# A hybrid attention step on one core: one input tile requested earlier, and the first gated tiles prepared ahead of weight splits

## The chip, the cores and the metric

The kernel runs on one core of a Trainium2 chip. The metric is the device time of one execution in microseconds. The median of the kernel before is 1729.63 us over 3 runs (1727.05 to 1729.91).

## What is computed

One layer of a decoder step in float32, for a prompt of 1024 rows and for 8 x 8 sampled rows. All rows are normalised and multiplied by one wide input matrix. Branch A is windowed attention in three dilations, branch B differential attention. Each branch output is gated, projected to 1024 columns, the projections are merged by sigmoid gates, and a last projection and the residual follow:

```python
h = rms_norm(x, norm_g); z = h @ w_in          # q, k, v of both branches, gates ga, gb, ma, mb
o_a = combine_groups(outs, lses)               # three dilated windows, weighted by their softmax sums
o_b = rms_norm(o_b, subln_g) * (1.0 - lam_init)
ya = o_a * silu(ga); yb = o_b * silu(gb)
pa = ya @ w_proj_a;  pb = yb @ w_proj_b
m = sigmoid(ma) * pa + sigmoid(mb) * pb
y = x + m @ w_out
```

## The kernel before

The program is written out by hand for each engine: five instruction streams (SP for transfers, GpSimd, ScalarE, VectorE, TensorE), ordered among themselves by semaphores only. An engine works strictly in the order of its stream, so an instruction that waits holds all that stand behind it. Rows come in 9 tiles: eight of 128 prompt rows (0 to 7) and one of the 64 sampled rows (8).

**Products in three parts.** A float32 product is made from rounded high and low parts: `hi*w_hi`, `hi*w_lo`, `lo*w_hi` (L2000 to L2002, and L2052 to L2054 for the gate units). So each weight chunk, 128 x 512 and 256 KB, is loaded into one of four `raw` buffers, ScalarE rounds it to `w_hi` (`split_hi`, L1195), and GpSimd (`split_lo`, L985) or VectorE (L1513) subtracts to make `w_lo`. A raw buffer is loaded again only when the `w_lo` of the chunk four before is done; in the late part of the kernel it is ScalarE that waits for this and issues the load (L1187, L1188), right behind a split.

**The start.** Chunks 0 to 7 are those of the first block of input weights. An input tile goes: load into one of two `xt` buffers (L704, `load_x`), `Square` with a row sum on ScalarE (L1206), reciprocal root on GpSimd (L965, L966), scaling on VectorE (`rows_scale`, L1520), eight transposes on TensorE (L1948), gain on VectorE (`hn`, L1529), high part on ScalarE (L1182), low part on GpSimd (L972). `load_x(i)` for i >= 2 waits until `rows_scale(i - 2)` is done. SP's order is: tile 0, two constants, tile 1, chunks 0 to 3, tile 2, chunks 4 to 7 (each behind the `w_lo` of the chunk four before), four small `qcol` loads, then, in `block_io(0)`, one tile and one chunk of the next block in turn, starting with tile 3. VectorE's order there is: `w_lo` of chunk 4, `rows_scale(2)`, `w_lo` of chunks 5 to 7, `rows_scale(3)`, `input_gain(2, 0)`; ScalarE's: split of chunks 4 to 7, square of tile 3, the high parts of tile 2. The second half of tile 2 is transposed by TensorE behind the first tile's products; that transposition waits for `input_gain(2, 0)`.

**The seam.** The decode part runs over groups `gg` = 0 to 70 (`SLOTS` is 70), and between its pieces the gate units (0 to 59) are multiplied. The last units stand at the end: in `gg` = 70 TensorE does unit 57, transposes `zyA` of tile 0 (`turn_y(0, 0)`, L1980), does unit 58, transposes `zyB` of tile 0, does unit 59 (16 products, the sampled rows), and goes on to `project(0, 0)`. From there its order is, for each tile i: `project(0, i)`, `turn_y(0, i+1)`, `project(1, i)`, `turn_y(1, i+1)`, with the transposes of the merged rows (`turn_m`) behind it.

In groups 64 to 69 two chunks a group of the projection weights are split (`late_splits`); those of `w_proj_a` have their low part made on VectorE, the first four of `w_proj_b` on GpSimd, in groups 68 and 69; chunk 4 of it stands ahead of unit 57. Chunks 5, 6, 7 of `w_proj_b` and the first of `w_out` (here called chunks 5 to 8) come behind group 70; 5 and 7 belong to GpSimd, 6 and 8 to VectorE.

The gated rows of a tile are prepared in two branches. Branch a: three attention outputs `ogA` and the gate `sgA` are loaded (L895, L900); GpSimd weights two of them and adds (`y_prepare_a`, L1110 twice, L1112), VectorE weights the third, adds and multiplies by the gate (`y_a`, L1764, L1766, L1770), which gives `zyA`. Branch b: `ogB` and `sgB` are loaded; ScalarE squares (`square`, L1388), GpSimd multiplies by the norm's weight and makes the reciprocal root (`y_prepare_b`, L1117, L965, L966), VectorE reduces, scales and multiplies by the gate (`y_b`, L1775, L1778, L1781), which gives `zyB`. After the transposition ScalarE moves the high part (`move_y`, L1392) and VectorE makes the low part (`y_low`, L1785), on which `project` waits. SP loads the pieces of the next tile of a branch when `zyA` or `zyB` of the one before is done (`load_y`). VectorE multiplies the projections by the merge gates (`gated`, L1806), two steps for each tile and branch.

Of the kernel before, what the change touches and what calls it, by code (L numbers as in the profile page):

```python
# [133 lines left out]
def build_step(nc, x_p, x_s, ca, cb, page_table, norm_g, w_in, qna, kna, qnb, knb, lq1, lk1, lq2, lk2,  # L134
# [17 lines left out]
    with ExitStack() as ctx:  # L152
# [378 lines left out]
        def splits_at(gg):  # L531

            return [q for q in sorted(split_slot) if split_slot[q] == gg]
# [162 lines left out]
        def _(sp):  # L696
# [22 lines left out]
            load_x(2)  # L719
            for k in range(4, KC):  # L720
                load_chunk(0, k)
            for col, vec in ((0, qna), (1, qnb)):
                for h in range(2):
                    sp.dma_start(qcol[h * HD:(h + 1) * HD, col:col + 1],
                                 vec[0].rearrange("(d o) -> d o", o=1)).then_inc(s_const, 16)
# [9 lines left out]
            def block_io(u):  # L735
                kind, G = U[u][0], U[u][1]
                for i in range(TILES):
                    if u == 0 and 3 <= i + 3 < TILES:
                        load_x(i + 3)
                    if u == 0 and i == NT - 1:  # L740
                        constants()
                    if i < KC:
                        load_chunk(u + 1, i)
                    if kind == "k":
                        kk = TILES * G + i
                        dst = kept(G, i, 0) if i < NT else kept_new(G, 0)
                        if dst is not None:
                            sp.wait_ge(kn_ready, kk + 1)
                            sp.dma_start(dst, kn[0:nrows(i), kk % 3, :])\
                                .then_inc(k_out[kk % 3], 16)  # L750
                            if i == NT:
                                sp.dma_start(new_scr[0, :, (G - 1) % 4], kn[0:NS, kk % 3, :])\
                                    .then_inc(k_out[kk % 3], 16)
                    if kind == "v" and G == 0 and i == NT:
                        sp.wait_ge(lo_done, first_chunk[4])
                        table_b(0)
                        table_b(1)
                    if kind == "v" and G and i == 5:
                        sp.wait_ge(k_out[2], k_sent[2][TILES * G + NT])
                        table_in(G, 0)  # L760
                    if kind == "v":
                        dst = kept(G, i, 1) if i < NT else kept_new(G, 1)
                        if dst is not None:
                            sp.wait_ge(v_ready, TILES * G + i + 1)
                            sp.dma_start(dst, v_sb[0:nrows(i), i, :]).then_inc(v_out, 16)
                            if i == NT:
                                sp.dma_start(new_scr[1, :, (G - 1) % 4], v_sb[0:NS, NT, :]).then_inc(v_out, 16)
# [184 lines left out]
        def _(pool):  # L952
# [183 lines left out]
            for gg in range(SLOTS + 1):  # L1136
# [6 lines left out]
                if n == 4 and b + 1 < DEC_B:  # L1143
# [1 line left out]
                    pool.wait_ge(*lo_ready(last_split[0]))  # L1145
                    queries(b + 1, slice(2, 4)).then_inc(s_qa, 1)
                    pool.wait_ge(s_qa, b + 2)
                if gg == SLOTS - 1:
                    y_prepare_a(0)
                for q in (*splits_at(gg), *late_splits(gg)):  # L1150
                    if not by_vector(q):
                        split_lo(*divmod(q, KC))
                if gg == SLOTS:
                    y_prepare_b(0)
                for m in gates_at(gg):
                    splits_for(m)
            def splits_of(chunks):
# [2 lines left out]
                        split_lo(*divmod(q, KC))  # L1160

            y_prepare_a(1)
            splits_of(range(Q_PB + NC + SPARE, Q_OUT + SPARE))
            for i in range(TILES):
                if i + 1 < TILES:
                    if i:
                        y_prepare_a(i + 1)
                    y_prepare_b(i + 1)
                if i:
                    merge(i - 1)  # L1170
# [7 lines left out]
        def _(act):  # L1178
# [228 lines left out]
            for gg in range(SLOTS + 1):  # L1407
# [38 lines left out]
                if gg == N_GROUPS + 3:  # L1446
                    act.wait_ge(ew_exp, 1)
                    act.activation(ew[:, :, :, :], ew[:, :, :, :], ACT.Exp).then_inc(ew_exp, 1)
                for q in splits_at(gg):
                    split_hi(*divmod(q, KC))  # L1450
                if gg == SLOTS:
                    act.wait_ge(s_pu, 9 * DEC_B)
                    square(0)
                for m in gates_at(gg):
                    gate(m)
                    if gg == SLOTS and m < GATE_UNITS - 1:
                        move_y(m - (GATE_UNITS - 3), 0)
                for q in late_splits(gg):
                    split_hi(*divmod(q, KC))
            for q in range(Q_PB + NC + SPARE, Q_OUT + SPARE):  # L1460
                split_hi(*divmod(q, KC))

# [7 lines left out]

            for i in range(TILES):
                if i + 1 < TILES:
                    square(i + 1)
                    move_y(0, i + 1)
                else:
                    halves(i, 0)
# [23 lines left out]
        def _(dve):  # L1500
# [397 lines left out]
                        split_lo(*divmod(q, KC))  # L1898

            y_a(1)  # L1900
            splits_of(range(Q_PB + NC + SPARE, Q_OUT + SPARE))
            for i in range(TILES):
                if i:
                    gated(1, i - 1)
                if i + 1 < TILES:
                    if i:
                        y_a(i + 1)
                    y_b(i + 1)
                gated(0, i)
                if i + 1 < TILES:  # L1910
# [506 lines left out]
```

## Time and profile before

| | |
|---|---|
| median of 3 runs | 1729.63 us (1727.05 to 1729.91) |
| the profiled execution, its own time | 1733.43 us |
| its span | 1731.6 us |
| TensorE products, busy | 1641.2 us (95%) |
| VectorE / GpSimd / ScalarE busy | 723.8 / 664.3 / 602.0 us |
| mean granted clock of TensorE | 0.987 |

The span is the profiled stretch from its first to its last instruction; the execution's own time has a little more around it. Matmuls are pipelined and overlap, so a busy TensorE is not one at its peak. The granted clock is 1.00 at 2.4 GHz and 0.50 at 1.2 GHz; a window that has both shows a mean. An idle time in brackets is that of the engine just before the instruction, with the step that ended it.

### The profile page before, as it was taken

How to read it: one execution, taken by the hardware profiler on the slowest of the kernel's cores; microseconds unless marked ns; L12 is line 12 of the kernel's file. 1: busy time of each engine (PE TensorE's matmuls, PEld its weight loads, DVE VectorE, ACT ScalarE, POOL GpSimd, SP SyncE). 2: the span in 40 equal slices, each digit the busy share in tenths (PEclk: the TensorE clock that was granted, in tenths of full speed). 3: DMA queues.
4: the chain of work that ended last, by engine and by line, in shares of the span. 5: the costliest groups of instructions: out<-in, count | busy, mean ns of one | idle time of the engine just before them, and what ended most of it. 6: DMA issues, size and time to landing. Idle time of an engine off the chain costs nothing.

```text
span 1731.6 us, 38772 instructions
## 1 busy us (share of the span) xinstructions
PE 1641.2 (95%) x14872; PEld 1406.5 (81%) x14872; DVE 723.8 (42%) x1788; ACT 602.0 (35%) x1405; POOL 664.3 (38%) x958
## 2 busy tenths in 40 slices
PE   6999888999999999999999999999999899999998
PEld 5888565778799999899998887777777788878787
DVE  5521556322174221642216463444354342478511
ACT  4422465422164221642217243334243344311300
POOL 5666110257452475524656131211221111466500
PEclk9999999999999999999999999999999999999999
DMA  5164710564814667344532789989899887755422
GB/s 159 56 221 160 251 51 0 164 202 170 272 50 135 205 232 245 116 158 163 195 114 70 257 274 297 309 281 320 277 317 310 279 284 236 256 182 177 151 91 79
DMA packets 184062, 336.27 MB, mean 194 GB/s; under 512 B 29969, under 2 KB 74130, under 8 KB 177746
## 3 DMA queue, kind: packets, MB, share of 16 engines
q1 hardware_dynamic: 143586, 221.68, 39.4%
q10 hardware_dynamic: 40304, 112.22, 19.2%
q8 instruction: 117, 1.92, 0.4%
q14 instruction: 55, 0.45, 0.1%
HBM read 294.05 MB, written 127.07 MB: 243 GB/s over the span
## 4 chain that ended last, share of the span: by engine, by line
PE 89%; issue 3%; DMA 2%; ACT 2%; DVE 2%; SPq 1%; POOL 1%; ACTq 0%; DVEq 0%; POOLq 0%
PE ps L2000 14%; PE ps L2002 14%; PE ps L2001 14%; PE ps L2052 5%; PE ps L2053 5%; PE ps L2054 5%; PE ps L2207 4%; PE ps L2151 4%; PE ps L2100 4%; PE ps L2171 3%; PE ps L2266 3%; PE ps L2249 2%; PE ps L2158 2%; PE ps L2121 2%; PE ps L1969 2%
## 5 line engine op out<-in xcount | busy, mean ns | idle before, releaser
L985 POOL TENSOR_TENSOR w_lo<-raw,w_hi 128x512 fp32r<-128x512 f32 x140 | 180.2, 1293 | 446.5 <-ACT w_hi L1195 445.9
L2000 PE MATMUL ps<-w_hi,hT 128*128 128x512 f32 x824 | 341.0, 414 | 2.0 <-POOL hT L972 1.0
L2002 PE MATMUL ps<-w_hi,hT 128*128 128x512 f32 x824 | 330.5, 401 | 0.0
L2001 PE MATMUL ps<-w_lo,hT 128*128 128x512 f32 x824 | 330.2, 401 | 0.0
L2000 PEld LDWEIGHTS ps<-w_hi,hT 128*128 128x128 f32 x824 | 206.2, 250 | 21.2 <-issue 1.4
L2052 PE MATMUL ps<-w_hi,hT 128*128 128x256 f32 x768 | 221.8, 289 | 1.6 <-issue 1.2
L2053 PE MATMUL ps<-w_lo,hT 128*128 128x256 f32 x768 | 217.2, 283 | 6.2 <-issue 6.2
L2002 PEld LDWEIGHTS ps<-w_hi,hT 128*128 128x128 f32 x824 | 206.5, 251 | 20.5
L2001 PEld LDWEIGHTS ps<-w_lo,hT 128*128 128x128 f32 x824 | 206.8, 251 | 18.1
L2054 PE MATMUL ps<-w_hi,hT 128*128 128x256 f32 x768 | 216.7, 282 | 0.0
L1195 ACT ACTIVATE w_hi<-raw 128x512 fp32r<-128x512 f32 x158 | 98.8, 629 | 200.2 <-DMA raw<-in_w_in 185.4
L2052 PEld LDWEIGHTS ps<-w_hi,hT 128*128 128x128 f32 x768 | 147.2, 192 | 9.9 <-issue 9.1
L2053 PEld LDWEIGHTS ps<-w_lo,hT 128*128 128x128 f32 x768 | 147.3, 192 | 3.6 <-issue 3.6
L2054 PEld LDWEIGHTS ps<-w_hi,hT 128*128 128x128 f32 x768 | 147.0, 191 | 3.2 <-issue 3.2
L1719 DVE STREAM_TRANSPOSE k_in<-k_in 128x512 f32<-128x512 f32 x224 | 138.1, 677 | 1.8 <-DMA k_in<-in_cache_a_kv 1.7
L1038 POOL TENSOR_SCALAR qz<-qT 64x128 f32<-64x128 f32 x208 | 109.2, 525 | 63.4 <-PE ps L2151 52.1
L966 POOL TENSOR_TENSOR rs<-ss,half_pow 128x8 f32<-128x8 f32 (+3 forms) x81 | 127.0, 1568 | 6.7
L1584 DVE TENSOR_REDUCE ss<-ps 128x8 f32<-128x512 f32 (+1 forms) x72 | 49.7, 690 | 172.1 <-ACT ps L1265 172.1
L1265 ACT ACTIVATE ps<-ps 128x512 f32<-128x512 f32 (+1 forms) x72 | 41.8, 580 | 213.6 <-PE ps L2002 206.2
L1597 DVE TENSOR_TENSOR zn<-ps,rs 128x512 f32<-128x512 f32 (+1 forms) x72 | 49.7, 690 | 141.9 <-POOL rs L966 141.9
L2151 PE MATMUL ps<-kT,qz 128*128 128x128 f32 (+1 forms) x384 | 101.3, 350 | 5.0 <-POOL qz L1038 3.5
L1326 ACT ACTIVATE sA<-sA,st_sum 128x128 f32<-128x128 f32 (+1 forms) x192 | 86.2, 449 | 42.5 <-DVE st_sum L1685 36.6
(233 smaller groups left out, 2863.1 us busy)
## 6 DMA issues: line engine op xcount, KB each, us to landing
out<-in_cache_a_kv ACTq DMA_DIRECT2D x29, 2040.0 KB, 9.3
k_in<-in_cache_b_kv SPq DMA_DIRECT2D x128, 256.0 KB, 3.8
v_in<-in_cache_b_kv SPq DMA_DIRECT2D x128, 256.0 KB, 6.2
raw<-in_w_in SPq DMA_DIRECT2D x104, 256.0 KB, 4.1
k_in<-in_cache_a_kv SPq DMA_DIRECT2D x104, 256.0 KB, 6.5
v_in<-in_cache_a_kv SPq DMA_DIRECT2D x104, 256.0 KB, 6.7
out<-in_cache_a_kv ACTq DMA_DIRECT2D x7, 2016.0 KB, 8.9
raw<-in_w_in ACTq DMA_DIRECT2D x40, 256.0 KB, 5.7
```

Of the source, the lines that this page charges most:

```text
L966: return pool.tensor_tensor(out, in_, half_pow[0:r, 0:heads], ALU.pow)
L985: pool.tensor_tensor(lo, raw_of(q), hi.bitcast(F32), ALU.subtract).then_inc(lo_done, 1)
L1038: return pool.tensor_scalar(out, in_, 1.0, None, ALU.mult)
L1195: act.activation(weights(q)[0], raw_of(q), ACT.Copy).then_inc(hi_done, 1)
L1719: dve.transpose(k_in[:, gg % NKS, j, :], k_in[:, gg % NKS, j, :]).then_inc(s_kt, 1)
L2000: pe.matmul(z, hi, wh, start=first, stop=False)
L2001: pe.matmul(z, hi, wl, start=False, stop=False)
L2002: return pe.matmul(z, lo, wh, start=False, stop=last)
L2052: pe.matmul(part, hi, wh, start=k == 0, stop=False)
L2053: pe.matmul(part, hi, wl, start=False, stop=False)
L2054: ins = pe.matmul(part, lo, wh, start=False, stop=k == KC - 1)
L2151: pe.matmul(bank(s % 4)[:, 0:W], qz[:, hh, i * P:(i + 1) * P], kT[:, k0:k0 + W], start=True, stop=True).then_inc(aq, 1)
```

## The change

Three engines and SP get another order; no instruction is added and none removed.

- SP: `load_x(3)` is issued behind chunk 5 of the first block, ahead of chunks 6 and 7 and of the `qcol` loads. `block_io(0)` then begins its tiles with 4.
- GpSimd: `y_prepare_a(0)` moves from group 69 to group 68, and in either group it stands ahead of that group's splits. `y_prepare_b(0)` stays in group 70 and is written ahead of that group's splits. `y_prepare_b(1)` moves ahead of the splits of chunks 5 to 8, to where `y_prepare_a(1)` already stands.
- ScalarE: in group 70, `square(0)` is written ahead of the splits; `square(1)` moves ahead of the splits of chunks 5 to 8.
- VectorE: `y_b(1)` moves ahead of the splits of chunks 5 to 8, behind `y_a(1)`.

```diff
--- before.py
+++ after.py
@@ -719,6 +719,8 @@
             load_x(2)
             for k in range(4, KC):
                 load_chunk(0, k)
+                if k == 5:
+                    load_x(3)
             for col, vec in ((0, qna), (1, qnb)):
                 for h in range(2):
                     sp.dma_start(qcol[h * HD:(h + 1) * HD, col:col + 1],
@@ -735,7 +737,7 @@
             def block_io(u):
                 kind, G = U[u][0], U[u][1]
                 for i in range(TILES):
-                    if u == 0 and 3 <= i + 3 < TILES:
+                    if u == 0 and 4 <= i + 3 < TILES:
                         load_x(i + 3)
                     if u == 0 and i == NT - 1:
                         constants()
@@ -1145,13 +1147,13 @@
                     pool.wait_ge(*lo_ready(last_split[0]))
                     queries(b + 1, slice(2, 4)).then_inc(s_qa, 1)
                     pool.wait_ge(s_qa, b + 2)
-                if gg == SLOTS - 1:
+                if gg == SLOTS - 2:
                     y_prepare_a(0)
+                if gg == SLOTS:
+                    y_prepare_b(0)
                 for q in (*splits_at(gg), *late_splits(gg)):
                     if not by_vector(q):
                         split_lo(*divmod(q, KC))
-                if gg == SLOTS:
-                    y_prepare_b(0)
                 for m in gates_at(gg):
                     splits_for(m)
             def splits_of(chunks):
@@ -1160,11 +1162,11 @@
                         split_lo(*divmod(q, KC))
 
             y_prepare_a(1)
+            y_prepare_b(1)
             splits_of(range(Q_PB + NC + SPARE, Q_OUT + SPARE))
             for i in range(TILES):
-                if i + 1 < TILES:
-                    if i:
-                        y_prepare_a(i + 1)
+                if 0 < i < TILES - 1:
+                    y_prepare_a(i + 1)
                     y_prepare_b(i + 1)
                 if i:
                     merge(i - 1)
@@ -1446,17 +1448,18 @@
                 if gg == N_GROUPS + 3:
                     act.wait_ge(ew_exp, 1)
                     act.activation(ew[:, :, :, :], ew[:, :, :, :], ACT.Exp).then_inc(ew_exp, 1)
-                for q in splits_at(gg):
-                    split_hi(*divmod(q, KC))
                 if gg == SLOTS:
                     act.wait_ge(s_pu, 9 * DEC_B)
                     square(0)
+                for q in splits_at(gg):
+                    split_hi(*divmod(q, KC))
                 for m in gates_at(gg):
                     gate(m)
                     if gg == SLOTS and m < GATE_UNITS - 1:
                         move_y(m - (GATE_UNITS - 3), 0)
                 for q in late_splits(gg):
                     split_hi(*divmod(q, KC))
+            square(1)
             for q in range(Q_PB + NC + SPARE, Q_OUT + SPARE):
                 split_hi(*divmod(q, KC))
 
@@ -1470,7 +1473,8 @@
 
             for i in range(TILES):
                 if i + 1 < TILES:
-                    square(i + 1)
+                    if i:
+                        square(i + 1)
                     move_y(0, i + 1)
                 else:
                     halves(i, 0)
@@ -1898,13 +1902,13 @@
                         split_lo(*divmod(q, KC))
 
             y_a(1)
+            y_b(1)
             splits_of(range(Q_PB + NC + SPARE, Q_OUT + SPARE))
             for i in range(TILES):
                 if i:
                     gated(1, i - 1)
-                if i + 1 < TILES:
-                    if i:
-                        y_a(i + 1)
+                if 0 < i < TILES - 1:
+                    y_a(i + 1)
                     y_b(i + 1)
                 gated(0, i)
                 if i + 1 < TILES:
```

## Rows read from the trace of the kernel before

**Rows 1.** The page's chain that ended last: shares of the span by engine.

```profile
PE 89%; issue 3%; DMA 2%; ACT 2%; DVE 2%; SPq 1%; POOL 1%; ACTq 0%; DVEq 0%; POOLq 0%
```

**Rows 2.** Windows of the start: busy time of each engine, granted clock (PEclk).

```profile
25.00:30.00 5.00, 2.06 (x9) 1.73 (x10) 2.04 (x3) 1.79 (x5) 2.04 (x3) 0.90 0.64 214
30.00:35.00 5.00, 5.00 (x23) 4.07 (x21) 3.03 (x4) 2.64 (x5) 4.71 (x5) 0.76 0.15 59
```

**Rows 3.** Timeline of the start: start us, length us, engine, line, instruction, [idle before <-releaser].

```profile
12.86 4.89 SPq L711 DMA_DIRECT2D raw<-in_w_in  x4
...
20.31 0.58 SPq L704 DMA_DIRECT2D xt<-in_x_prompt  x1
...
20.33 2.96 DVE L1513 TENSOR_TENSOR w_lo<-raw,w_hi 128x512 fp32r<-128x512 f32 x3
...
20.41 0.63 ACT L1195 ACTIVATE w_hi<-raw 128x512 fp32r<-128x512 f32 x1 [0.76 <-DMA raw<-in_w_in]
...
24.34 1.06 ACT L1206 ACTIVATE xn<-xt 128x1024 f32<-128x1024 f32 x1 [3.30 <-DMA xt<-in_x_prompt]
...
26.44 0.75 DVE L1520 TENSOR_SCALAR xn<-xt,rs_x 128x1024 f32<-128x1024 f32 x1 [3.15 <-POOL rs_x L966]
...
27.94 0.63 PE L1948 MATMUL ps<-ident,xn 128*128 128x128 f32 x4 [3.43 <-DVE hn L1529]
```

**Rows 4.** Windows of TensorE alone: products before and behind the seam's waits, with PEclk.

```profile
1485.49:1491.36 5.87, 5.86 (x49) 1.00 0.59 175
1495.91:1503.70 7.79, 7.79 (x52) 0.73 0.89 298
1511.78:1517.62 5.84, 5.84 (x27) 1.00 0.69 246
1521.83:1530.23 8.40, 8.40 (x26) 0.66 0.77 263
```

**Rows 5.** Timeline of the seam, GpSimd, VectorE, ScalarE, SP and TensorE.

```profile
1474.42 0.39 SPq L900 DMA_DIRECT2D sgA<-g_scr  x1
...
1485.49 2.61 POOL L985 TENSOR_TENSOR w_lo<-raw,w_hi 128x512 fp32r<-128x512 f32 x2 [29.07 <-ACT w_hi L1195]
...
1488.06 2.16 POOL L1110 TENSOR_TENSOR ogA<-ogA,ew 128x512 f32<-128x512 f32 x2
...
1490.30 1.28 POOL L1112 TENSOR_TENSOR ogA<-ogA 128x512 f32<-128x512 f32 x1
...
1491.54 2.94 POOL L985 TENSOR_TENSOR w_lo<-raw,w_hi 128x512 fp32r<-128x512 f32 x2
...
1491.69 1.66 DVE L1766 TENSOR_TENSOR ogA<-ogA 128x512 f32<-128x512 f32 x1 [5.99 <-POOL ogA L1112]
...
1493.38 1.64 DVE L1770 TENSOR_TENSOR zyA<-ogA,sgA 128x512 f32<-128x512 f32 x1
...
1494.44 1.72 POOL L1117 TENSOR_TENSOR ogB<-ogB,subrow 128x512 f32<-128x512 f32 x1
...
1495.17 1.09 PE L1980 MATMUL ps<-ident,zyA 128*128 128x128 f32 x4 [3.82 <-DVE zyA L1770]
...
1507.64 0.69 DVE L1766 TENSOR_TENSOR ogA<-ogA 128x512 f32<-128x512 f32 x1
...
1513.46 0.63 ACT L1388 ACTIVATE zyB<-ogB 128x512 f32<-128x512 f32 x1 [1.32 <-POOL w_lo L985]
...
1516.88 1.52 DVE L1778 TENSOR_TENSOR ogB<-ogB,rs 128x512 f32<-128x512 f32 x1 [2.07 <-POOL rs L966]
...
1518.44 1.42 DVE L1781 TENSOR_TENSOR zyB<-ogB,sgB 128x512 f32<-128x512 f32 x1
...
1519.91 0.66 PE L1980 MATMUL ps<-ident,zyB 128*128 128x128 f32 x4 [2.29 <-DVE zyB L1781]
...
1521.83 0.80 PE L2000 MATMUL ps<-w,yT 128*128 128x512 f32 x1 [1.26 <-DVE yT L1785]
```

**Rows 6.** The tile view of `sgA`, its load issued at 1474.4.

```profile
DMA to landing us min/median/max: 9.8/9.8/9.8
```

## Prediction, made before the changed kernel ran

> **What bounds the kernel now.** I read the page's chain first: TensorE is 89% of it [rows 1], so a microsecond counts only where TensorE stands still or runs at its lower clock (1.2 instead of 2.4 GHz). The diff touches two places, the first 25 us and the seam between the gate units and the projections. There I read the granted clock by windows, then all engines' instructions in order of time.
>
> In the start, TensorE waits 3.43 us, until 27.94, for `hn` of tile 2, and the clock then falls for a while [rows 2, 3]. The reader is to follow that wait back: ScalarE's `Square` of tile 3 starts at 24.34, after 3.30 us idle for `xt`; that load was issued at 20.31, behind eight weight chunks and four `qcol` loads; VectorE, in order, holds tile 2's gain (L1529) behind `rows_scale(3)`, which starts at 26.44 [rows 3].
>
> In the seam TensorE waits 3.82 us for `zyA` of tile 0, 2.29 for `zyB` of tile 1 and 1.26 for its low part [rows 5], and each time the clock falls: the 48 products behind the first wait take 7.79 us against 5.87 before it, the 24 behind the others 8.40 against 5.84 [rows 4]. GpSimd is why: it makes two `w_lo` (1485.49, 2.61), then branch a (2.16 and 1.28), then two more `w_lo` (2.94), then branch b [rows 5].
>
> **Part 1, the fourth input tile.** `load_x(3)` moves ahead of chunks 6, 7 and the four `qcol` loads. Its wait, `h_xn` of tile 1, is long met, so it adds no stall to SP. The last four chunk issues span 12.86 to 17.75 [rows 3], so it goes out near 15.0 and, at the 4.0 us that this load took (20.31 to 24.34), is there by 19.3. ScalarE gets to it after the split of chunk 7 (20.41 + 0.63 = 21.04) and squares until 22.3; GpSimd's reciprocal root, the 1.0 us between that and 26.44 in the old order, ends at 23.3. VectorE is in its three `w_lo` until 20.33 + 2.96 = 23.29 [rows 3]. So `rows_scale(3)` starts near 23.4 instead of 26.44, the gain follows 0.7 us later, and the transpose at 24.85 instead of 27.94: 3.1 us. The mean clock of 0.90 and 0.76 in two stretches of 5 us [rows 2] is 0.5 + 1.2 = 1.7 us lost; TensorE stood still just before. With 0.35 us of wait left I take those back too. Sum 4.8, lower bound 3.1 (the clock falls anyway).
>
> Against it: 512 KB now go in front of chunks 6 and 7. Split 7 already waits 0.76 us for its chunk [rows 3]. A whole tile's 4.0 us is the ceiling; but chunk 6 is asked for one chunk request later (four of them took 4.89 us, so 1.2) and would overlap it. VectorE works on chunk 5 until 20.33 + 2.96 - 2 x 0.69 = 21.9, so 1 us of delay is covered and 2 us would cost 1 us. I take nothing and keep 1.5 for the range. The requests behind `qcol` move up by the tile's issue of 0.58 us [rows 3]; what they bring is needed later.
>
> **Part 2, branch a of tile 0 ahead of the splits.** `y_prepare_a(0)` moves one slot up, in front of four `w_lo`. It waits for `ogA`. No row gives that landing; the gate load issued behind it at 1474.42 landed after 9.8 us [rows 5, 6], so 1484.2 is the late bound, and I take 1483. GpSimd then needs 2.2 + 1.3 us and frees VectorE near 1486.6 instead of 1491.69. VectorE's two steps took 1.66 and 1.64 us beside GpSimd's splits, and 0.69 without them [rows 5]; they will again have splits beside them, so `zyA` is ready at 1490. Gate 57 ends at 1491.36 [rows 4]: the wait of 3.82 goes, and with it the slow clock (7.79 - 5.87 = 1.9, and 0.4 on the transposes, 1.09 against 0.66) [rows 4, 5].
>
> The Trainium skill (GPSIMD Engine Reference, Key points) says that GpSimd and VectorE share their SBUF interfaces, with contention when the VectorE instruction has two SBUF inputs. The pair of durations agrees (1.66 against 0.69), and by the rule alone it speaks against preparing on both engines at once. The sum already uses the long values.
>
> What the move delays: `w_lo` 0 and 1 of `w_proj_b` start at 1486.6 instead of 1485.49, 1.1 us. Behind them ScalarE asks for chunk 4 (needs `w_lo` 0), then copies the last decode output, splits 2 and 3, and asks for chunk 6 (needs `w_lo` 2). As branch a no longer stands between, `w_lo` 2 and 3 end at 1493.0 instead of 1494.5.
>
> **Part 3, branch b of tile 0.** Nothing else is in front of `square(0)` in its slot, so that edit alone is nothing. It starts when ScalarE has asked for chunk 6, at 1492.1. From the square of tile 1 to its `zyB` took 1513.46 to 1519.86, 6.4 us [rows 5]; so `zyB` of tile 0 is ready at 1498.4. TensorE transposes from 1491.2 on (four, 0.66 with their tail [rows 5]) and does gate 58 (48 products, 5.87 [rows 4]) until 1497.5. A new wait of 0.9 us.
>
> **Part 4, both branches of tile 1 ahead of the later splits.** With `zyA(0)` 5 us earlier, SP requests `ogA(1)` at 1490, and `ogB(1)` at 1498.4 (the second has branch b of tile 0 in front). Gate 59 (16 products of the same width, a third of 5.87) ends at 1500.9, project(0,0) takes 5.84 [rows 4] to 1506.7. On ScalarE `square(1)` stands behind gate 59's three steps and starts near 1502.9; with the same 6.4 `zyB(1)` is there at 1509.3, and it is wanted after project(1,0), at 1512.6. The wait of 2.29 goes. The splits of chunks 5 to 8 now stand behind it on three engines. From the square to the step that uses the root took 1516.88 - 1513.46 = 3.4 us [rows 5], so GpSimd has the `w_lo` of chunk 5 from 1506.3 to 1507.6; VectorE that of chunk 6 from 1509.3 to 1510.6; ScalarE's request and split of chunk 8 follow that, and VectorE's `w_lo` of it ends at 1512.3. project(1,0) wants chunk 6 at 1510.7: nothing lost, and nothing to spare. Then VectorE does `gated(0,0)` (two steps) and `y_low(0,1)`, three of 0.69, ready at 1514.3 where TensorE wants it at 1513.1: a wait of 1.2 where there were 1.26. With the waits goes the clock loss, 8.40 - 5.84 = 2.6 us [rows 4].
>
> Seam: 3.8 + 2.3 + 2.3 + 1.3 + 2.6 = 12.3 that is there, less 0.9 + 1.2 = 2.1 of new waits: 10.2. After that each projection tile has the same work on each engine as before, and no wait stood there.
>
> By the Trainium skill (TensorE: Matmul & The Clock Gate, PE-mode transpose), transposes do not count as work for the clock as products do. By it the new wait of 0.9 us is 1.5 with the four transposes behind it; if the clock fell for that, the seam would give 7.9. No row here shows a fall behind so short a stop.
>
> **Sum.** 4.8 + 10.2 = 15.0. The profiled execution took 1733.43 (its span 1731.6 and 1.8 around it): 1718.4. The median of the runs shown is 3.8 lower, 1729.63, which gives 1714.6; I predict 1714.6.
>
> **Rivals.**
> - *The new waits grow.* The chain to `zyB(0)` crosses three engines and chunk requests; at 2.2 us more (each VectorE and GpSimd step at its long duration, or `ogA` at its late bound), TensorE waits 3.1 us before transposing branch b, the clock falls again (2.3), and project(1,0), with nothing to spare, waits as well: 2.2 more and 2.6 of clock. 15.0 - 2.2 - 2.3 - 2.2 - 2.6 = 5.7: 1724; one of the two, 1719. For it: long durations in every row with both engines busy [rows 5]. Against: the forecast already has the long durations in most places.
> - *The tile in front of chunks 6 and 7 costs what it gives.* The first tile's last products come 2 to 3 us later, the clock falls anyway; the start gives 0 to 1.5, the whole some 11: 1719.
> - *It doesn't do what it says.* Both waits end last on something else (landing of `xt` with the chunks in front; decode's last copy on ScalarE): within 3 us of 1729. Against: both releasers in the trace are the steps moved [rows 3, 5].
> - *Slower: GpSimd stands at `y_prepare_a(0)`.* Four splits, ScalarE's chunk requests and all later stand behind this one wait. It decides only if it eats 15.0 and 3.5 more, so if `ogA` lands after 1483 + 18.5 = 1501.5, 27 us after its last issue, where the load behind it took 9.8 [rows 6]. At 1506 it gives 1737.6.
>
> **How the numbers follow.** Chances: forecast 0.60, growing waits 0.20, start lost 0.10, nothing 0.06, slower 0.04. What a measurement here can tell from no change is 0.2%, 3.5 us. Lower end of the range: no new waits (17.2 us), 1712.4, and 2.4 for execution to execution (the runs shown differ by 2.9); upper end: the first rival in full, 1724. The forecast's own range is 1711 to 1718.5, from no new waits to the clock at the start falling anyway and 2 us of waits more. Faster 0.91 (with the cases of 5 us and more, and a piece of "nothing"), same 0.05, slower 0.04.
>
> **What would show it.** `xt` of tile 3 issued near 15 and its square near 21; TensorE's wait for `hn` under 0.6, clock 1.00 in 25 to 35. In the seam GpSimd's L1110 ahead of four L985; no wait of TensorE for `zyA`; waits for `zyB(0)` and `y_low(0,1)` near 1 us; clock 1.00 throughout. Wrong if a wait over 2 us stands at gate 59 or at project(0,1), or if the split of chunk 7 starts after 22.

## The result and the profile after

Over 18 runs of each kernel in turn, the median went from 1734.86 to 1722.28 us. The ratio is 0.9931 with a 95% interval of 0.9912 to 0.9949: 12.0 us faster (8.8 to 15.3). The profiled execution of the changed kernel took 1716.18 us, its span is 1714.3.

A span alone says little here: single executions of one kernel lie 11 to 19 us apart. So I cut each span at four landmarks of TensorE: the first product, the last transposition of an input row tile, the sum that ends the decode part, and the first transposition of a merged tile. In the changed kernel they are these (timeline, TensorE):

```profile
13.40 0.77 PE L2004 MATMUL ps<-w_hi,hT 128*128 128x512 f32 x1 [1.04 <-POOL hT L974]
...
64.56 0.46 PE L1952 MATMUL ps<-ident,xn 64*128 64x64 f32 x4
...
1477.52 0.41 PE L2282 MATMUL ps<-om,sel 128*32 128x128 f32 x2 [0.48 <-DVE om L1887]
...
1518.78 0.60 PE L1994 MATMUL ps<-ident,sig 128*128 128x128 f32 x4
```

In the kernel before the same four stand at 14.10, 69.37, 1485.15 and 1536.52. That gives, in us:

| stretch | before | after | difference | predicted |
|---|---|---|---|---|
| up to the first product | 14.1 | 13.4 | 0.7 | 0 |
| start: to the last input transposition | 55.27 | 51.16 | 4.1 | 4.8 |
| middle: to the last decode sum | 1415.8 | 1413.0 | 2.8 | 0 |
| seam: to the first merged transposition | 51.37 | 41.26 | 10.1 | 10.2 |
| tail: to the end of the span | 195.1 | 195.5 | -0.4 | 0 |

Start and seam together gave 14.2 us, which lies inside the interval of the ratio, 8.8 to 15.3. How well do such stretches repeat? The start of the old order stood between 55.04 and 55.27 in the five profiles that have it unchanged, that of the new between 51.14 and 51.16 in five (and 51.14 in a sixth, with the tile one place further up, part 5). The old seam took 51.37, 50.70, 50.09 and 52.05 in four, with the waits of [rows 5], but for one of 0.8 instead of 1.26 in the third, and a clock of 0.87 to 0.90; the new one 41.26, 41.52 and 41.80 in three. By these means it gives 9.5 us; 10.1 is the pair of the two profiles. The differences in the first row and in the middle are ones that executions of any of these kernels have among themselves (the middle ran from 1407.5 to 1422.7 over the 14 profiles of this study), and are put down to nothing in the change.

**The start.** Timeline of the changed kernel, SP, ScalarE, GpSimd, VectorE, TensorE; compare [rows 3]:

```profile
14.20 0.43 SPq L704 DMA_DIRECT2D xt<-in_x_prompt  x1
15.52 1.53 SPq L711 DMA_DIRECT2D raw<-in_w_in  x2
...
18.91 0.63 ACT L1197 ACTIVATE w_hi<-raw 128x512 fp32r<-128x512 f32 x1 [1.11 <-DMA raw<-in_w_in]
19.89 0.63 ACT L1197 ACTIVATE w_hi<-raw 128x512 fp32r<-128x512 f32 x1 [0.35 <-DMA raw<-in_w_in]
20.43 1.04 ACT L1208 ACTIVATE xn<-xt 128x1024 f32<-128x1024 f32 x1
...
21.65 0.37 POOL L967 TENSOR_SCALAR ss_x<-ss_x 128x1 f32<-128x1 f32 x1 [0.84 <-ACT xn L1208]
22.10 0.88 POOL L968 TENSOR_TENSOR rs_x<-ss_x,half_pow 128x1 f32<-128x1 f32 x1
...
23.02 0.75 DVE L1524 TENSOR_SCALAR xn<-xt,rs_x 128x1024 f32<-128x1024 f32 x1 [0.45 <-POOL rs_x L968]
...
24.52 0.63 PE L1952 MATMUL ps<-ident,xn 128*128 128x128 f32 x4 [0.74 <-DVE hn L1533]
```

The square of tile 3 has no idle time in front of it: the tile was there before ScalarE had done the last split. What is left of TensorE's 3.43 us is 0.74: of the 4.1 us that the start gained, 2.7 are this wait and 1.4 the clock behind it. Windows, all engines, with the granted clock (compare [rows 2]):

```profile
25.00:30.00 5.00, 5.00 (x29) 4.09 (x27) 2.02 (x4) 2.77 (x6) 4.51 (x5) 1.00 0.40 144
30.00:35.00 5.00, 5.00 (x29) 4.04 (x27) 4.89 (x7) 2.19 (x5) 3.54 (x4) 1.00 0.13 29
```

**The seam.** Timeline, GpSimd, VectorE, ScalarE and TensorE; compare [rows 5]:

```profile
1474.82 2.16 POOL L1112 TENSOR_TENSOR ogA<-ogA,ew 128x512 f32<-128x512 f32 x2 [25.87 <-DMA ogA<-o_scr]
...
1478.29 3.44 POOL L987 TENSOR_TENSOR w_lo<-raw,w_hi 128x512 fp32r<-128x512 f32 x2
...
1478.91 1.66 DVE L1770 TENSOR_TENSOR ogA<-ogA 128x512 f32<-128x512 f32 x1
1480.61 1.67 DVE L1774 TENSOR_TENSOR zyA<-ogA,sgA 128x512 f32<-128x512 f32 x1
...
1483.90 0.63 ACT L1390 ACTIVATE zyB<-ogB 128x512 f32<-128x512 f32 x1 [1.07 <-POOL w_lo L987]
...
1489.17 1.42 DVE L1785 TENSOR_TENSOR zyB<-ogB,sgB 128x512 f32<-128x512 f32 x1
...
1490.73 0.63 PE L1984 MATMUL ps<-ident,zyB 128*128 128x128 f32 x4 [0.96 <-DVE zyB L1785]
...
1495.11 0.63 ACT L1390 ACTIVATE zyB<-ogB 128x512 f32<-128x512 f32 x1 [0.59 <-ACT stage L1379]
...
1503.10 1.58 DVE L1517 TENSOR_TENSOR w_lo<-raw,w_hi 128x512 fp32r<-128x512 f32 x1 [1.13 <-ACT w_hi L1197]
1504.71 1.29 DVE L1810 TENSOR_TENSOR sig<-sig,ps 128x512 f32<-128x512 f32 x2
...
1506.65 0.50 PE L2004 MATMUL ps<-w,yT 128*128 128x512 f32 x1 [1.38 <-DVE yT L1789]
```

Read the first line well: GpSimd now stands at `y_prepare_a(0)` until `ogA` has landed. It is released 2.7 us before the decode sum, so the standing costs nothing yet. Behind it, `zyA` of tile 0 is ready at 1482.28, while gate 57 still runs to 1483.6. The two waits that are left, 0.96 and 1.38, are the two that were forecast. Windows of TensorE alone (busy, granted clock), compare [rows 4]: gate 57, gate 58, gate 59 with project(0,0), and the stretch behind the last wait.

```profile
1477.86:1483.73 5.87, 5.87 (x51) 1.00 0.54 168
1483.92:1489.78 5.86, 5.86 (x51) 1.00 0.87 311
1491.12:1498.82 7.70, 7.70 (x45) 1.00 0.97 310
1506.65:1518.78 12.13, 12.13 (x57) 1.00 0.60 208
```

The granted clock is 1.00 (2.4 GHz) in all these windows, where 7.79 us stood at 0.73 and 8.40 at 0.66 before. And the chain of work that ended last has a new long piece, the landing of `ogA`:

```profile
1465.71 8.97 DMA ogA<-o_scr
```

### The profile page after: what moved, and what is told of

It is laid out like the page before. It is cut to its first block, busy times and chain, and to the rows that moved or that the text cites. A ratio compares the mean times of both kernels' runs of the same rounds, so it can differ in the third digit from the quotient of the medians.

```text
span 1714.3 us, 38772 instructions
## 1 busy us (share of the span) xinstructions
PE 1635.2 (95%) x14872; PEld 1403.0 (82%) x14872; DVE 721.2 (42%) x1788; ACT 601.4 (35%) x1405; POOL 665.7 (39%) x958
## 4 chain that ended last, share of the span: by engine, by line
PE 88%; DMA 3%; issue 3%; SPq 2%; ACT 2%; DVE 1%; POOL 1%; ACTq 0%; DVEq 0%; POOLq 0%
PE ps L2004 14%; PE ps L2006 14%; PE ps L2005 14%; PE ps L2056 5%; PE ps L2057 4%; PE ps L2058 4%; PE ps L2155 4%; PE ps L2211 4%; PE ps L2104 4%; PE ps L2175 3%; PE ps L2270 3%; PE ps L2162 2%; PE ps L2253 2%; PE ps L1973 2%; PE ps L2125 2%
## 5 line engine op out<-in xcount | busy, mean ns | idle before, releaser
L967 POOL TENSOR_SCALAR ss<-ss 128x8 f32<-128x8 f32 (+3 forms) x81 | 15.8, 196 | 222.8 <-DVE ss L1588 202.4
```

## The experiments

"Start" and "seam" below are the two stretches of the table. They come from one profiled execution each; times of five rounds are beside them where there are any.

### 1. The tile alone, the seam alone

The first is the kernel before with the edit of SP's order only; the second is the changed kernel with SP's order as before.

```diff
# tile alone, against the kernel before
                 load_chunk(0, k)
+                if k == 5:
+                    load_x(3)
...
-                    if u == 0 and 3 <= i + 3 < TILES:
+                    if u == 0 and 4 <= i + 3 < TILES:
```

> Only the fourth input tile is requested earlier; the seam is as before. My theory: the time from TensorE's first product (14.10 us in the trace of before) to the last transposition of an input tile (69.4) shrinks from 55.3 by 4 to 5 us, to 50.5 to 51.5, with the clock at 1.00 in 25 to 35 us, and the seam's three waits (3.8, 2.3, 1.3 us) stand as they were. Rival, the tile costs chunks 6 and 7 what it gives: below 1.5 us. In the time: 0.9972 to 0.9976 of before by the theory, 1.000 by the rival; the whole change gave 0.9931.

> Only the seam's orders are changed; the start is as before, with its wait of 3.4 us and the slow clock behind it. My theory: from the last sum of the decode part (1485.15 in before) to the first transposition of merged rows (1536.5) 51.4 shrinks to 41.3, with new waits of about 1.0 and 1.4 us; 0.9941 of before. Rival, the seam's gain comes with the start's by chance of phase and is given back elsewhere: 0.997 or more.

| | ratio to before (95%) | start | seam |
|---|---|---|---|
| tile alone | 0.9981 (0.9959 to 1.0003) | 51.15 | 50.70 |
| seam alone | 0.9948 (0.9925 to 0.9970) | 55.04 | 41.52 |
| both (the change) | 0.9931 (0.9912 to 0.9949) | 51.16 | 41.26 |

Each part does its own work, and these numbers show no effect of one on the other. By the ratios they give 3.3 us (-0.5 to 7.1) and 9.0 (5.2 to 13.0), 12.3 together, where both gave 12.0. The tile's part cannot be told from nothing by its time alone; its stretch of the profile shows it, 4.1 us shorter. With the tile alone the seam has its three old waits of 3.8, 2.3 and 1.3. TensorE's waits in the seam of the kernel without the tile (line, releaser, us in total, times, longest):

```profile
PE ps L2002 <- DVE yT L1787: 1.4, 1, 1.4
PE ps L1982 <- DVE zyB L1783: 1.2, 1, 1.2
```

### 2. The seam in halves: tile 0 and tile 1

The kernel before with `y_prepare_a(0)` one group earlier (the new wait for `zyB` of tile 0 is 0.96 us with it, as in the change, so the other edits for tile 0 show no effect), and the kernel before with only the edits of tile 1.

```diff
# tile 0
-                if gg == SLOTS - 1:
+                if gg == SLOTS - 2:
                     y_prepare_a(0)
# tile 1
             y_prepare_a(1)
+            y_prepare_b(1)
...
+            square(1)
             for q in range(Q_PB + NC + SPARE, Q_OUT + SPARE):
...
             y_a(1)
+            y_b(1)
```

> Of the seam only branch a of tile 0 moves ahead of four splits on GpSimd. My theory: the wait for zyA (3.8 us) and the slow clock behind it (2.3) are gone and a wait of about 1 us for zyB of tile 0 comes; the two later waits of TensorE (2.3 and 1.3 us) stay or grow a little, as nothing of tile 1 is ahead of its splits; landmark distance 51.4 to about 46. Rival, the two halves are one chain, so that half of the edit only moves the wait on: 49 or more.

> Of the seam only branch b of tile 1 moves ahead of the splits of chunks 5 to 8, on three engines. My theory: the wait for zyA of tile 0 stays 3.8 us with the slow clock; the wait for zyB of tile 1 (2.3) goes, that for its low part stays at 1 to 2 us; the clock stays full there; landmark distance 51.4 to about 46.5. Rival, with tile 0 late its chain now holds the splits and project(1, 0) waits for chunk 6: a new wait of 2 us or more, distance above 49.

TensorE alone, seam stretch of the kernel before, of tile 0, of tile 1 (us, busy, granted clock, DMA share, GB/s):

```profile
1485.15:1536.52 51.37, 43.99 (x235) 0.87 0.60 197
```

```profile
1477.71:1522.94 45.23, 40.71 (x235) 0.96 0.68 224
```

```profile
1487.82:1533.47 45.65, 40.47 (x234) 0.96 0.69 222
```

Tile 0 gives 6.1 us, tile 1 gives 5.7; together they would be 11.9 (6.14 and 5.72), and the change gave 10.1, each of these to within about 1 us by the scatter of the old seam. The waits show why. With tile 0's step alone the first is gone, but the transpositions of `zyB` now wait twice; with tile 1's alone the second is gone:

```profile
PE ps L1980 <- DVE zyB L1781: 3.3, 2, 2.3
PE ps L2000 <- DVE yT L1785: 1.3, 1, 1.3
```

```profile
PE ps L1982 <- DVE zyA L1772: 3.8, 1, 3.8
PE ps L2002 <- DVE yT L1787: 1.4, 1, 1.4
```

The sum in the first line holds the new wait of 1.0 for branch b of tile 0 (3.3 less 2.3), as forecast. Taking the waits out of the sums leaves the clock: tile 0 gave 6.1 for 3.8 - 1.0 = 2.8 of waits, so 3.3 by the clock; tile 1 gave 5.7 for 2.3 - 0.1 = 2.2 of waits, so 3.5. Both halves together gave 10.1 for 3.8 + 2.3 - 1.0 - 0.1 = 5.0 of waits, so 5.1. The clock's part of the halves is 6.8 and that of both is 5.1.

The traces show where these 1.7 us come from. In each half one old wait stayed as long as it was, but the slow products behind it ended sooner. TensorE alone: tile 0's kernel behind its waits of 2.3 and 1.3, then tile 1's behind its wait of 3.8; compare the 8.40 at 0.66 and the 7.79 at 0.73 of [rows 4]:

```profile
1509.22:1516.62 7.40, 7.40 (x26) 0.77 0.78 251
1498.23:1505.62 7.39, 7.39 (x53) 0.77 0.88 282
```

With the transposes in front of the second, these are 1.00 and 0.75 us less than before, 1.75 together. That is the whole difference between the sum of the halves and the change. So these profiles show no loss from having both; what differs between executions is the price in clock of one and the same wait. In the five profiles that have the old wait of 3.8, the slow products behind it lasted 2.3 to 5.1 us, and in the five that have those of 2.3 and 1.3 (once 0.8) 3.2 to 6.1.

### 3. The clock without the waits

The kernel before, with products added that nothing reads, so that TensorE has work while it waits: 14 ahead of `turn_y(0, 0)`, 8 and 4 around `turn_y(1, 1)`. Nothing is left out of the computation, and no step of another engine is moved.

```diff
+                    pe.wait_ge(s_tb, DEC_B)
+                    fill(0, 14)
                     turn_y(0, 0)
...
                 project(1, i)
+                if i == 0:
+                    pe.wait_ge(gs, GATE_UNITS)
+                    fill(6, 8)
                 if i + 1 < TILES:
                     turn_y(1, i + 1)
+                if i == 0:
+                    fill(6, 4)
```

> The kernel before, with TensorE's waits in the seam filled by products whose result nobody reads (14 of 512 columns ahead of the first transposition of zyA, 8 and 4 around that of zyB of tile 1). Nothing that TensorE waits for comes earlier, so only the clock can change. My theory, that 4.9 of the 12.3 us in the seam were the clock and not the wait: the clock stays at 1.00 and the landmark distance falls from 51.4 to about 46.5. Rival, that the products behind a wait are slow for another reason (contention, refilling of weights): 51 or more.

TensorE in the seam's stretch:

```profile
1489.59:1536.17 46.58, 45.18 (x260) 1.00 0.66 211
```

The clock is 1.00 and the stretch is 4.8 us shorter. The transposition of `zyA` of tile 0 comes no sooner, 10.0 us behind the decode sum in both. That of `zyB` of tile 1 does, 32.5 us behind it where it was 34.8: the gate units in front of it run at the full clock, and ScalarE gets to `square(1)` sooner. So the expectation that nothing TensorE waits for comes earlier was wrong for tile 1, and part of the 4.8 reaches the time by this way. The prediction's sum had 2.3 + 2.6 = 4.9 for the clock. The same 4.8 is what a kernel gets here that only keeps TensorE busy; the other 5.3 of the 10.1 needs the earlier steps.

### 4. What holds the start: the load, or VectorE's order

In the old order `input_gain(2, 0)` stands behind `rows_scale(3)`. One could leave SP alone and swap the two on VectorE; or do both.

```diff
-            rows_scale(3)
             input_gain(2, 0)
+            rows_scale(3)
             input_gain(2, 1)
```

> The kernel before, with VectorE's input_gain(2, 0) ahead of rows_scale(3) and the tile requested as late as before. The first transposition then no longer stands behind the late tile on VectorE. My theory (the load sets the pace of everything behind it): the wait of 3.4 us is gone at this place but the next one, for xn or hn of tile 3, takes most of it back, as rows_scale(3) still starts near 26.4 and TensorE wants it near 26.5 plus its transposition; distance from first product to last input transposition 55.1 to between 51 and 53. Rival, only VectorE's order was wrong: 51.2 or less, as good as the earlier load, without any wait.

> The kernel before with the early fourth tile (as in the kernel with part 1 alone) and input_gain(2,0) ahead of rows_scale(3) on VectorE; the seam as before. Theory (with the tile early the gain's only remaining cause for a wait is the 0.45 us that rows_scale(3) stands for the root, plus its own 0.75): the wait for hn of 0.7 us goes, the stretch from the first product to the last input transposition is 50.3 to 50.8 us instead of 51.15. Rival (what the swap takes from hn of tile 2 it gives to tile 3, as it did without the early tile, where the wait only moved to the next transposition): 51.0 to 51.8.

The swap alone made the start 54.23, which is 1.0 us less and outside both what the theory (51 to 53) and what the rival expected: less came of it than either said. Its largest wait went from 3.4 to 2.7 us and stands at the next transposition, for the gain behind the late `rows_scale(3)`; the clock in the window from 25 to 30 was 0.74. The wait:

```profile
PE ps L1948 <- DVE hn L1529: 2.7, 1, 2.7
```

Tile and swap together made it 50.23, 0.9 shorter than the tile alone, and no wait for `hn` is left. So the late load was the cause, and the order on VectorE worth 0.9 us more once the load is early; on its own it mostly moves the wait.

### 5. The place among the chunks

One rival was that 512 KB in front of chunks 6 and 7 hold these up. If so, the tile in front of all four must hold up more. Against the changed kernel:

```diff
             load_x(2)
+            load_x(3)
             for k in range(4, KC):
                 load_chunk(0, k)
-                if k == 5:
-                    load_x(3)
```

> The changed kernel with load_x(3) right behind load_x(2), ahead of all of chunks 4 to 7 instead of behind chunk 5. Theory (the 512 KB of the tile hold up what is asked for behind them by a request's slot of about 1.2 us and more): VectorE's and ScalarE's splits of chunks 4 and 5 start 1 to 2 us later, TensorE waits in the first tile's products for w_lo, and the stretch from the first product to the last input transposition is 52 to 53.5 us instead of 51.16. Rival (the transfers overlap enough that the place of the tile among the chunks does not matter): 51.0 to 51.4.

The start was 51.14, the same as with the tile behind chunk 5. ScalarE's waits for its chunks were two, and they sum to 1.3 us, where the changed kernel had 1.11 + 0.35:

```profile
ACT w_hi L1196 <- DMA raw<-in_w_in: 1.3, 2, 0.9
```

My theory fell, the rival was right: between these two places the order of the requests does not matter to the start.

### 6. What the two waits that are left are made of

The 1.38 us for `y_low(0, 1)`: VectorE makes the low part of the first chunk of `w_out` in front of it (1503.10, 1.58 us), which TensorE does not want for long. In the next kernel ScalarE's split and VectorE's low part of that chunk stand behind tile 1's first half (VectorE's edit; ScalarE's is of the same kind):

```diff
-            splits_of(range(Q_PB + NC + SPARE, Q_OUT + SPARE))
+            splits_of(range(Q_PB + NC + SPARE, Q_OUT))
...
                     y_low(0, i + 1)
+                    if i == 0:
+                        splits_of(range(Q_OUT, Q_OUT + SPARE))
                     y_low(1, i + 1)
```

> The changed kernel, with chunk 8 (the first of w_out, not wanted for 100 us) split behind the move and the low part of tile 1's branch a, on ScalarE and VectorE. My theory: the wait of 1.4 us for the low part is the queue behind chunk 8 on VectorE and goes to 0.3 or less; landmark distance 41.3 to 40.0. Rival, gated(0, 0) or the move on ScalarE is what is late: 41 or more.

The seam was 39.09, 2.2 us under the change. The wait for `y_low(0, 1)` is gone, and of TensorE's waits behind the decode sum one of 0.5 is left:

```profile
PE ps L1988 <- DVE zyB L1787: 0.5, 1, 0.5
```

This wait lies ahead of what the edit moves, and was 0.96, 1.18 and 1.46 in the three profiles of the change's own seam. So 0.5 of the 2.2 us is a difference between executions, and the edit gives 1.7.

The 0.96 us for `zyB` of tile 0: in ScalarE's stream `square(0)` stands behind the splits of group 69, and `y_prepare_b(0)` behind GpSimd's. Here it and `y_prepare_b(0)` move one group up, against the changed kernel:

```diff
-                if gg == SLOTS:
+                if gg == SLOTS - 1:
                     y_prepare_b(0)
...
-                if gg == SLOTS:
+                if gg == SLOTS - 1:
                     act.wait_ge(s_pu, 9 * DEC_B)
                     square(0)
```

> The changed kernel with branch b of tile 0 one group earlier: square(0) and y_prepare_b(0) stand ahead of the splits of group 69 instead of group 70. Theory (the wait of 1.0 us for zyB of tile 0 that the change left is ScalarE's place in its stream, not the load of ogB): the wait goes, the stretch from the last decode sum to the first merged-row transposition is 40.0 to 40.8 us instead of 41.26, and 1.4 for y_low(0,1) stays. Rival (the stream is full: what moves forward pushes the w_lo of w_proj_b back): the wait goes but one of 1 us or more appears at gate 59 or project(0,0), and the stretch is 41.3 to 43.

The wait for `zyB` went, and three came: the seam was 43.85, 2.6 us over the change. The rival was right, and the seam even passed its range of 41.3 to 43. TensorE's waits, and ScalarE's timeline:

```profile
PE ps L2004 <- DVE yT L1789: 2.1, 1, 2.1
PE ps L1984 <- DVE zyA L1774: 1.3, 1, 1.3
PE ps L2004 <- DVE w_lo L1517: 0.8, 1, 0.8
```

```profile
1493.28 0.63 ACT L1197 ACTIVATE wx<-raw 128x512 fp32r<-128x512 f32 x1 [3.64 <-POOL w_lo L987]
...
1494.98 0.60 ACT L1379 ACTIVATE stage<-ps 128x512 f32<-128x512 f32 x1 [1.07 <-POOL w_lo L987]
...
1497.16 0.38 ACTq L1361 DMA_DIRECT2D m_scr<-stage  x1
...
1502.18 0.38 ACT L1377 ACTIVATE stage<-ps 64x256 f32<-64x256 f32 x1 [4.00 <-DMA m_scr<-stage]
```

Branch b on GpSimd now stands in front of two `w_lo`; ScalarE, asking for the chunks, waits 3.64 us for them, and so takes gate 57 out 11.2 us behind the decode sum instead of 7.6. Gates 57 and 58 are then stored one right behind the other (1494.98 and 1496.54), and gate 59's copy finds its stage buffer, one of two, still being written out: 4.00 us. Everything behind it, `square(1)` first, is 2.6 us late. The slack of the changed kernel on ScalarE lay in the distance between these copies.

### 7. How late may the attention pieces come

GpSimd's wait for `ogA` was the slower rival. SP here asks for the pieces of tile 0 only when gate 56 is done:

```diff
+            sp.wait_ge(gs, GATE_UNITS - 3)
             load_y(0, 0)
             load_y(1, 0)
```

> The changed kernel, with the load of tile 0's branch pieces held back on SP until gate 56 is through ScalarE, some 11 us later than now (near 1476.6 instead of 1464.7). It prices the slower rival: GpSimd stands at y_prepare_a(0) with four splits behind it. My theory: the pieces land 3 to 5 us behind their issue, as the queue is by then short, so y_prepare_a(0) starts 5 to 6 us later; zyA comes back as a wait of 4 us or more before its transposition, the clock falls, the four splits and the chunk requests slip too; distance 41.3 to 49 to 52. Rival, the slack in front of GpSimd takes it: below 44.

GpSimd's timeline:

```profile
1493.10 2.60 POOL L1113 TENSOR_TENSOR ogA<-ogA,ew 128x512 f32<-128x512 f32 x2 [35.35 <-DMA ogA<-o_scr]
```

That is 6.3 us behind the decode sum (1486.76), where it was 2.7 ahead of it: 9.0 us later. I had expected 5 to 6; the pieces, asked for from 1485.90 on, were there only after 7.2 us and not after 3 to 5. The seam was 50.18, 8.9 longer, with 7.7 us of wait for `zyA`. At this lateness the price is about one to one, and the seam's whole gain but 1.2 is gone. The placement of the change rests on this, that `ogA` is asked for at 1465.71 and lands 8.97 us later, ahead of the decode sum.

### 8. What was found, put together

The changed kernel with the swap of part 4 and both edits of part 6. It was set down before the result of branch b's move was known.

> The changed kernel with three further swaps: input_gain(2,0) ahead of rows_scale(3); branch b of tile 0 ahead of the splits of group 69; the first chunk of w_out split behind move_y(0,1) and y_low(0,1). Theory (the waits left are places in the streams, and add up): start 50.6 us instead of 51.16, seam 38.5 us instead of 41.26, together 3.3 us less than the changed kernel, a ratio to the kernel before of 0.989 to 0.993, that is 1713 to 1719 us beside a kernel before of 1732. Rival (each swap only moves its wait): start 51 or more, seam 39 or more, ratio 0.992 to 0.995.

The start was 50.22, as expected; the seam 41.19, not 38.5. Its waits show the two edits of part 6 at work against each other, the one for `yT` gone, the two that branch b's move brings still there:

```profile
PE ps L2008 <- DVE w_lo L1519: 0.8, 1, 0.8
PE ps L1988 <- DVE zyA L1776: 0.6, 1, 0.6
```

Its median over 6 runs was 1715.87 us, the ratio to the kernel before 0.9889 (0.9861 to 0.9917). It is faster than the kernel before, by 19.3 us (14.4 to 24.1); that it beats the change as well is likely by the ratios, whose intervals just touch, though the two stretches give it only 1.0 us. Where the rest comes from, if it is there, stays open. The version that the experiments point to, this one without the move of branch b, was not run; its two stretches, 50.2 and 39.1, would be 3.1 us under the change, of which 0.5 is the short wait of part 6 that the edit does not make.

## Why the prediction was right

**The time.** 15.0 us were forecast and the two stretches gave 14.2; by the ratio it was 12.0 (8.8 to 15.3). The median of the changed kernel, 1722.28, lies in the range of 1710 to 1724 but above the forecast's own range. It lies 7.7 us over the forecast of 1714.6. Of these, 5.2 are the median of before from which the sum was taken: 1729.63 from 3 runs, 1734.86 from 18. On the latter the forecast would have been 1719.9. That the time still fell inside the range is owed to its upper end, which stands for a rival that did not happen; the gains, not the absolute time, are what the prediction had right.

**The start: right, 0.7 us too large.** 4.8 were forecast, 4.1 came. The steps held: tile asked for between chunks, square with no wait, clock 1.00. The term that was mis-sized is the wait left over: 0.35 was taken, 0.74 stood. The prediction let `rows_scale(3)` follow VectorE's last `w_lo` almost at once; it had to wait 0.45 for the root. That is 0.4 of the 0.7; the other 0.3 is the clock, taken at 1.7 from the granted clock of two windows, where behind the transposition the start gained 1.4. From the start of GpSimd's first step to the end of its second took 1.33 us (21.65 to 22.98), where the kernel before has 0.82, GpSimd's timeline:

```profile
25.58 0.19 POOL L965 TENSOR_SCALAR ss_x<-ss_x 128x1 f32<-128x1 f32 x1 [4.04 <-ACT xn L1206]
25.85 0.55 POOL L966 TENSOR_TENSOR rs_x<-ss_x,half_pow 128x1 f32<-128x1 f32 x1
```

In the old order VectorE was idle then; in the new one it makes `w_lo` beside them. The prediction used the long durations for VectorE's steps beside GpSimd's and forgot them for GpSimd's beside VectorE's, which even at 128x1 elements are 0.37 and 0.88 for 0.19 and 0.55. That the clock stayed up with 0.74 of wait was the larger risk, and it held in all six profiles that have this wait with the early tile.

**Chunks 6 and 7: right at nothing.** Split 6 waited 1.11 us and split 7 0.35, but the last `w_lo` ended at 22.57, ahead of the root. Part 5 shows that even a tile in front of all four costs nothing. The 1.5 kept for the range was not needed.

**The seam: right, 10.1 for 10.2.** Counted from the decode sum (1485.15 before, 1477.52 after), in us:

| step | forecast | measured |
|---|---|---|
| GpSimd starts branch a of tile 0 | -2.15 | -2.70 |
| `zyA` of tile 0 ready | 4.85 | 4.76 |
| `square(0)` | 6.95 | 6.38 |
| `zyB` of tile 0 ready | 13.25 | 13.07 |
| `square(1)` | 17.75 | 17.59 |
| `zyB` of tile 1 ready | 24.15 | 23.84 |
| `w_lo` of chunk 8 ends | 27.15 | 27.16 |
| wait for `zyB(0)` | 0.9 | 0.96 |
| wait for `y_low(0,1)` | 1.2 | 1.38 |

(The forecast has the times of the prediction, the measured column those of the trace.) The choice that carried this was to take VectorE's steps beside GpSimd's at their long durations; they took 1.66 and 1.67 us again, and 0.69 where GpSimd was idle. The contention of the two engines that the Trainium skill describes (GPSIMD Engine Reference, Key points) is there, in both kernels alike. It does not decide against the change, because `zyA` has 1.3 us to spare, but it has a share in the two waits that are left: VectorE's two steps to `zyB` of tile 0 took 1.78 and 1.42, and its `w_lo` of chunk 8 took 1.58, where such steps take 0.69 alone.

That the sum came out to 0.1 is in part luck: it was worked out from the very profile with which it is compared, and by the means of four old and three new profiles the seam gives 9.5.

**The clock: 4.9 forecast, 4.8 by the filled kernel, 5.1 by the sum of part 2.** The rule of the Trainium skill (TensorE: Matmul & The Clock Gate, PE-mode transpose), by which transposes do not count as work for the clock, was weighed by the prediction, with 7.9 for the seam. The windows behind the 0.96 us wait and its four transposes are at 1.00, so it did not bite here; whether it is true of longer stretches of transposes, no run here shows.

**The rivals.** Growing waits: not here, but part 6 shows how near they were. One group further up, and ScalarE loses 2.6 us and the seam with it. The tile costing what it gives: no, by part 5. Doing nothing: no, by part 1. The slower one: GpSimd did stand at `ogA`, but 2.7 us ahead of the decode sum. Part 7 gives its price at one point, 8.9 us for 9 us late, which would have left the whole change a gain still. The 18.5 us late from which the prediction let it end slower than before agrees with that price, but no run was as late.

**What stays open.** The middle part, in which the change does nothing, differs by up to 15 us between the profiles, where the start of one order differs by 0.2, the seam by 2 and the tail by 1.6: it is nearly all of their scatter. Two profiles of nearly equal kernels, the tile alone (1407.5) and the seam alone (1420.9), show nearly half of their 13.4 us in TensorE's idle time that waits for nothing that the profile shows (called "issue"): at its two largest lines 11.2 and 5.0 us against 15.0 and 7.1, 5.9 together. Another 5.6 is TensorE being busy longer with the same products (1350.2 against 1355.8 us, granted clock 1.00 against 0.99). What varies behind "issue" was not looked for.

## What to carry to other kernels

Where an in-order engine prepares operands and splits weights in one stream, move the preparation up to just behind the landing of its data, and count who then waits for the splits: the step taken here gave 10.1 us, the next one of the same kind took 2.6. The three waits of together 7.4 us cost almost 5 us more in slow clock, and work that merely fills them gave 4.8 us. And where single executions scatter by more than the gain, cut the span at landmarks: here the stretches repeated to 0.2 us in the start and to 2 in the seam, while the middle moved by 15. Expect the clock's part of a wait to scatter: the same wait of 3.8 us was followed by 2.3 to 5.1 us of slow products.

## What the runs showed of the hardware that I had not expected

- In the start and the seam the granted clock stayed at 1.00 behind waits of TensorE of 0.74, 0.96, 1.38, 1.46 (part 5) and, with 1.25 and 0.83 ahead of it, 2.07 us (the kernel of part 6 with branch b moved). It fell behind 2.7, 3.4 and 3.8 us, and in the seam where 2.29 and 1.26, or 2.29 and 0.80 (the swap of part 4 alone), follow each other.
- A tile of 512 KB requested ahead of two or of four 256 KB chunks left the last of ScalarE's splits at nearly the same place, 6.5 and 6.3 us behind the first product, where it started 6.3 behind it without the tile.
- Contention of VectorE and GpSimd is not read off from overlap alone, as one of the two can keep its short duration. In the changed kernel GpSimd's `w_lo` at 1498.80 took 1.29 us and VectorE's scaling, begun at 1498.87 beside it, 1.77; VectorE's last step to `zyA` at 1495.60 took 0.69 and GpSimd's step begun at 1495.82 took 1.64. In these two pairs the step that began first was the short one. Where both began at 1501.28, VectorE's `w_lo` took 0.68 and GpSimd's 1.84.
